# Up-products with 512-column and 256-column matmuls in turns, in a twelve-part transformer kernel

## The reference

```python
# mlp, 4 times; w1 is 1024x4096, w2 is 4096x1024
x = x + rms_norm(sq_relu_mlp(rms_norm(x, g2), w1, w2), g3)   # jnp.square(jax.nn.relu(h @ w1)) @ w2
# ffn1 and ffn2, twice each; gate and up are 1024x2816, down is 2816x1024
x = x + 0.5 * swiglu(rms_norm_2(x, norm), w_gate, w_up, w_down)  # (silu(h @ w_gate) * (h @ w_up)) @ w_down
```

## Time and profile before

| | |
|---|---|
| median of 3 runs | 2692.18 us (2687.8 to 2705.8) |
| span of the profiled execution | 2705.3 us (0.5 under the highest run; the page gives no time outside the span) |
| PE busy | 2625.5 us (97%), 21582 matmuls |
| PEld busy | 2553.7 us (94%) |
| DVE busy | 1660.7 us (61%) |
| ACT busy | 1351.4 us (50%) |
| granted TensorE clock, mean | 0.993 |
| DMA | 451.96 MB, 167 GB/s |

### The profile page before, as it was taken

The page is one execution under the profiler, slowest core; times in us unless marked ns, Lnnn a source line. Parts: engine busy times, 40 slices in busy tenths (PEclk is TensorE's granted clock), DMA queues, the critical chain, the costliest instruction groups (busy, mean ns, idle before and its releaser), DMA issues.

```text
span 2705.3 us, 48788 instructions
## 1 busy us (share of the span) xinstructions
PE 2625.5 (97%) x21582; PEld 2553.7 (94%) x21582; DVE 1660.7 (61%) x1970; ACT 1351.4 (50%) x1663; POOL 152.2 (6%) x224
## 2 busy tenths in 40 slices
PE   8989999999998999989999999999999999999998
PEld 8979999899997999988999999989999999999998
DVE  5657655475575754676755665766665657764664
ACT  5645545454436544663544444554545446544543
POOL 4400000000000000330000000000000000000000
PEclk9999999999999999999999999999999999999999
DMA  7514564456643565442565756434766655334663
GB/s 214 162 33 141 187 234 133 152 176 211 211 144 121 179 219 186 144 147 94 171 216 178 191 187 211 152 125 141 196 194 187 189 199 159 126 130 142 188 188 125
DMA packets 429970, 451.96 MB, mean 167 GB/s; under 512 B 13346, under 2 KB 395024, under 8 KB 427584
## 3 DMA queue, kind: packets, MB, share of 16 engines
q1 hardware_dynamic: 417952, 416.12, 49.2%
q0 software_dynamic: 7312, 32.35, 3.5%
q10 hardware_dynamic: 4496, 0.39, 0.1%
HBM read 441.21 MB, written 7.60 MB: 166 GB/s over the span
## 4 chain that ended last, share of the span: by engine, by line
PE 85%; DVE 6%; ACT 4%; POOL 2%; DMA 1%; issue 1%; ACTq 0%; SPq 0%; DVEq 0%
PE ps L593 85%; ACT wH L1440 2%; DVE wL L2064 2%; POOL arena L497 1%; ACT hidden_parts L1500 1%; PE ps L1037 0%; POOL arena L499 0%; DMA ring<-in_gdn_w_in 0%; DVE arena L2484 0%; DMA arena<-tiles_out 0%; DVE arena L2592 0%; DMA arena<-leaf_out 0%; DMA leaf_out<-arena 0%; POOL arena L507 0%; DVE arena L2335 0%
## 5 line engine op out<-in xcount | busy, mean ns | idle before, releaser
L2064 DVE TENSOR_TENSOR wL<-ring,wH 128x2048 fp32r<-128x2048 f32 x392 | 898.4, 2292 | 781.2 <-ACT wH L1440 780.8
L1440 ACT ACTIVATE wH<-ring 128x2048 fp32r<-128x2048 f32 x392 | 752.4, 1919 | 1050.6 <-PE ps L593 1048.6
L593 PE MATMUL ps<-hidden_parts,wH 128*128 128x256 f32 x6656 | 1005.0, 279 | 4.1 <-ACT hidden_parts L1500 2.7
L593 PEld LDWEIGHTS ps<-hidden_parts,wH 128*128 128x128 f32 x6656 | 910.8, 188 | 6.1 <-issue 3.6
L593 PE MATMUL ps<-hidden_parts,wL 128*128 128x256 f32 x3328 | 700.4, 279 | 1.0 <-DVE wL L2064 1.0
L593 PEld LDWEIGHTS ps<-hidden_parts,wL 128*128 128x128 f32 x3328 | 525.4, 188 | 1.4 <-DVE wL L2064 1.4
L593 PE MATMUL ps<-hH,wH 128*128 128x256 f32 x2624 | 369.5, 282 | 7.1 <-DVE hH L2081 5.0
L593 PE MATMUL ps<-hH,wL 128*128 128x256 f32 x2624 | 361.6, 279 | 2.2 <-DVE wL L2064 2.2
L593 PEld LDWEIGHTS ps<-hH,wH 128*128 128x128 f32 x2624 | 331.4, 189 | 16.6 <-issue 15.9
L593 PE MATMUL ps<-hL,wH 128*128 128x256 f32 x2624 | 347.0, 278 | 0.0
L593 PEld LDWEIGHTS ps<-hH,wL 128*128 128x128 f32 x2624 | 329.2, 189 | 2.9 <-DVE wL L2064 2.8
(11 more groups left out here) (301 smaller groups left out, 1965.2 us busy)
## 6 DMA issues: line engine op xcount, KB each, us to landing
ring<-in_mlp_w SPq DMA_DIRECT2D x128, 1024.0 KB, 5.4
ring<-in_ffn_w_gate SPq DMA_DIRECT2D x88, 512.0 KB, 3.9
ring<-in_ffn_w_up SPq DMA_DIRECT2D x88, 512.0 KB, 5.2
ring<-in_ffn_w_down SPq DMA_DIRECT2D x44, 1024.0 KB, 5.0
ring<-in_gdn_w_in SPq DMA_DIRECT2D x32, 1024.0 KB, 5.9
ring<-in_w_in SPq DMA_DIRECT2D x28, 1024.0 KB, 5.4
hidden_parts<-mem_parts POOLq DMA_DIRECT2D x14, 1024.0 KB, 7.5
ring<-in_mlstm_w_in SPq DMA_DIRECT2D x12, 1024.0 KB, 5.2
```

Source lines behind the costliest of these rows:

```text
L593: return pe.matmul(o, l, r, start=start, stop=stop, **k)
L1440: f(wH[:, n % PARTS, :], ring[:, n % RING, :], ACT.Copy).then_inc(sem("high_split"), 1)
L2064: tt(wL[:, n % PARTS, :], ring[:, n % RING, :], wH[:, n % PARTS, :].bitcast(F32), ALU.subtract)\
```

## The change

Units 2 and up of the up-products go through one new function, `wide_product`. For each output m and each k it issues one matmul of wH's slice with 512 moving columns (xH and xL of chunk k side by side, a view of two pieces), into a whole PSUM bank, and then one of wL's slice with xH (256 columns) into the first half of that bank. So a unit has 16 matmuls of 512 columns and 16 of 256, and 32 weight loads in place of 48. A unit takes two banks, (0,1), (6,7) or (4,5) in turn. The two halves of a bank must still be added: ScalarE copies the xL halves of both banks into SBUF, and VectorE adds the xH halves to it. The wait for `low_split` moves to the head of the unit. In mlp the square of the Relu becomes a separate VectorE instruction on SBUF data. In ffn the scaling reads SBUF data. The wait for the filler's bank (6) moves from unit 2 to unit 3, and down-products wait until the unit before the last has been read. `hH` and `hL` become one tensor `normed`. At the start, the constants' first DMA and x share a semaphore, and the step semaphores are made when first used; the order of the work is not changed by that.

```diff
-        hH = sb("hH", [P, DC, T], F32R)
-        hL = sb("hL", [P, DC, T], F32R)
+        normed = sb("normed", [P, 2, DC, T], F32R)
+        hH, hL = normed[:, 0, :, :], normed[:, 1, :, :]
...
+        def wide_banks(j):
+            return (0, 6, 4)[(j - 2) % 3]
+
+        def both_sums(j):
+            v = ps[:, wide_banks(j):wide_banks(j) + 2, :]
+            return v[:, :, 0:T], v[:, :, T:2 * T]
...
+            def wide_product(u, j, high_of, low_of, x):
+
+                for m in range(2):
+                    bank = wide_banks(j) + m
+                    halves = two(ps[:, bank, :])
+                    if m == 0:
+                        pe.wait_ge(sem("low_split"), u + 1)
+                    for k in range(DC):
+                        mm(halves, high_of(k, m), x[:, :, k, :], k == 0, False, skip_group_check=True)
+                        last = mm(ps[:, bank, 0:T], low_of(k, m), x[:, 0, k, :], False, k == DC - 1,
+                                  skip_group_check=True)
+                last.then_inc(sem("products_done"), 1)
...
                 for j in range(2, 16):
-                    if j == 2:
+                    if j == 3:
                         filler_out(filled_before[("mlp", i)])
-                    to_channels("mlp_w1", i, j, bank_of(j), free="bank_read")
+                    if j == 4:
+                        pe.wait_ge(sem("hidden_squared"), W.next("hidden_squared", 2))
+                    if j >= 5:
+                        pe.wait_ge(sem("bank_read"), W.next("bank_read"))
+                    u = slab_no[("mlp_w1", i, j)]
+                    wh, wl = high(u, DC), low(u, DC)
+                    wide_product(u, j, lambda k, m: columns(wh, k, m), lambda k, m: columns(wl, k, m), normed)
                     if i == 0 and j == 3:
                         summed_norm(3, "xsq_summed")
+                W.next("hidden_squared", 14)
+                pe.wait_ge(sem("bank_read"), W.next("bank_read", 2))
...
+                    if n == 3:
+                        filler_out(filled_before[(kind, l)])
+                    if n == 4:
+                        pe.wait_ge(sem("units_scaled"), W.next("units_scaled", 2))
+                    if n >= 5:
+                        pe.wait_ge(sem("bank_read"), W.next("bank_read"))
                     u = slab_no[(kind, l, n)]
                     wh, wl = high(u, 2 * DC), low(u, 2 * DC)
-                    if n == 2:
-                        filler_out(filled_before[(kind, l)])
-                    if n >= 4:
-                        pe.wait_ge(sem("bank_read"), W.next("bank_read"))
-                    for half in range(2):
-                        last = three(ps[:, 4 + n % 4, half * T:(half + 1) * T],
-                                     [lambda k: wh[:, half * DC + k, :], lambda k: wl[:, half * DC + k, :]],
-                                     [lambda k: ffn_x[0][:, k, :], lambda k: ffn_x[1][:, k, :]], DC,
-                                     low_weights(u, (1, 0)) if half == 0 else None)
-                    last.then_inc(sem("products_done"), 1)
+                    wide_product(u, n, lambda k, m: wh[:, m * DC + k, :], lambda k, m: wl[:, m * DC + k, :], ffn_both)
+                W.next("units_scaled", 20)
+                pe.wait_ge(sem("bank_read"), W.next("bank_read", 2))
                 down_product(f"{kind}_w_down_2", l, 22, range(22))
...
-                    f(act_s[:, g % 2, :], ps[:, 4 + g % 4, :], ACT.Relu).then_inc(sem("act_ready"), 1)
+                    src = two(ps[:, 4 + g, :]) if g < 2 else both_sums(g)[1]
+                    f(two(act_s[:, g % 2, :]), src, ACT.Copy).then_inc(sem("act_ready"), 1)
...
+                    if n >= 2:
+                        f(two(sum_s[:, n % 2, :]), both_sums(n)[1], ACT.Copy).then_inc(sem("act_ready"), 1)
...
-                    tt(prod_s[:, g % 2, :], act_s[:, g % 2, :], ps[:, 4 + g % 4, :], ALU.mult)\
-                        .then_inc(sem("bank_read"), 1)
+                    src = act_s[:, g % 2, :]
+                    if g >= 2:
+                        tt(two(src), both_sums(g)[0], two(src), ALU.add).then_inc(sem("bank_read"), 1)
                     if g >= 1:
                         hidden_low(g - 1)
+                    if g >= 2:
+                        dve.wait_ge(sem("bank_read"), W.next("bank_read"))
+                    stt(prod_s[:, g % 2, :], src, 0.0, src, ALU.max, ALU.mult).then_inc(sem("hidden_squared"), 1)
...
-                    tt(two(act_s[:, n % 2, :]), two(ps[:, 4 + n % 4, :]), rs_twice(), ALU.mult)\
-                        .then_inc(sem("bank_read"), 1)
-                    dve.wait_ge(sem("bank_read"), W.next("bank_read"))
+                    src = ps[:, 4 + n, :] if n < 2 else sum_s[:, n % 2, :]
+                    if n >= 2:
+                        dve.wait_ge(sem("act_ready"), W.next("act_ready"))
+                        tt(two(src), both_sums(n)[0], two(src), ALU.add).then_inc(sem("bank_read"), 1)
+                        dve.wait_ge(sem("bank_read"), W.next("bank_read"))
+                    tt(two(act_s[:, n % 2, :]), two(src), rs_twice(), ALU.mult).then_inc(sem("units_scaled"), 1)
+                    dve.wait_ge(sem("units_scaled"), W.next("units_scaled"))
```

More of the change, by code:

```diff
@@ L206, in __init__ @@
             def __init__(self, eng, step):
-                self.eng, self.seen, self.step, self.steps = eng, {}, sem(step), 0
+                self.eng, self.seen, self.step, self.steps = eng, {}, step, 0
             def next(self, name, n=1):
@@ L216, in mark @@
                 self.steps += 1
-                ins.then_inc(self.step, 1)
+                ins.then_inc(sem(self.step), 1)
                 return self.steps
             def chain(self, ins):
-                self.eng.wait_ge(self.step, self.mark(ins))
+                self.eng.wait_ge(sem(self.step), self.mark(ins))
         def group(name, layer, j, g=0):
@@ L288, in program @@
         gate_s = A.take(2 * T, "p (b n) -> p b n", b=2)
+        sum_s = A.take(2 * 512, "p (b n) -> p b n", b=2)
         A = Arena()
@@ L330, in program @@
         memH, memL = hidden_parts[:, 0, 24:32, :], hidden_parts[:, 1, 0:8, :]
-        ffn_x = (hidH[:, 24:32, :], hidL[:, 24:32, :])
+        ffn_both = hidden_parts[:, :, 24:32, :]
+        ffn_x = (ffn_both[:, 0, :, :], ffn_both[:, 1, :, :])
         cross_x = [flat_parts[:, at:at + DC * T].rearrange("p (c t) -> p c t", c=DC)
@@ L391, in _ @@
         def _(sp):
-            sp.dma_start(ident, io["shape_constants"][:, 0:P]).then_inc(sem("ident_in"), 16)
+            sp.dma_start(ident, io["shape_constants"][:, 0:P]).then_inc(sem("x_in"), 16)
             sp.dma_start(x_rows, io["x"][0].rearrange("(i p) n -> p i n", p=P)).then_inc(sem("x_in"), 16)
@@ L869, in ffn @@
                 for n in range(2, 22):
+                    if n == 3:
[3 more added lines that the diff above has]
+                    if n >= 5:
+                        pe.wait_ge(sem("bank_read"), W.next("bank_read"))
                     u = slab_no[(kind, l, n)]
                     wh, wl = high(u, 2 * DC), low(u, 2 * DC)
-                    if n == 2:
-                        filler_out(filled_before[(kind, l)])
-                    if n >= 4:
-                        pe.wait_ge(sem("bank_read"), W.next("bank_read"))
-                    for half in range(2):
-                        last = three(ps[:, 4 + n % 4, half * T:(half + 1) * T],
-                                     [lambda k: wh[:, half * DC + k, :], lambda k: wl[:, half * DC + k, :]],
-                                     [lambda k: ffn_x[0][:, k, :], lambda k: ffn_x[1][:, k, :]], DC,
-                                     low_weights(u, (1, 0)) if half == 0 else None)
-                    last.then_inc(sem("products_done"), 1)
+                    wide_product(u, n, lambda k, m: wh[:, m * DC + k, :], lambda k, m: wl[:, m * DC + k, :], ffn_both)
+                W.next("units_scaled", 20)
+                pe.wait_ge(sem("bank_read"), W.next("bank_read", 2))
                 down_product(f"{kind}_w_down_2", l, 22, range(22))
-                pe.wait_ge(sem("bank_read"), W.next("bank_read", 4))
+                pe.wait_ge(sem("bank_read"), W.next("bank_read"))
             def outputs(heads, values):
@@ L1403, in turn_in @@
                     last.then_inc(sem(name), 1)
-            pe.wait_ge(sem("ident_in"), W.next("ident_in", 16))
             pe.wait_ge(sem("ones_set"), W.next("ones_set"))
-            pe.wait_ge(sem("x_in"), W.next("x_in", 16))
+            pe.wait_ge(sem("x_in"), W.next("x_in", 32))
             turn_in(x_rows, "x_turned")
@@ L1593, in hidden_high @@
             def hidden_high(g):
-                act.wait_ge(sem("bank_read"), W.next("bank_read"))
+                act.wait_ge(sem("hidden_squared"), W.next("hidden_squared"))
                 f(hidH[:, 2 * g:2 * g + 2, :], two(prod_s[:, g % 2, :]), ACT.Copy).then_inc(sem("hiddenH_ready"), 1)
@@ L1598, in gate_unit @@
                 def gate_unit(n):
```

(2 more changed lines are left out.)

3 lines of the change are left out of this document (1 added, 2 removed).

## The result

The changed kernel took 2737.55 us (median of 4 runs, 2733.62 to 2742.2) against 2695.67 for the kernel before (4 runs, 2687.8 to 2705.8): a ratio of 1.0154, 95% interval 1.0125 to 1.0183. It is slower by some 42 us, where 17 less were forecast. The forecast has the wrong sign, and the result lies outside its range.

The account below looks back on a forecast made before the run. PE was taken as the bound, busy 97% of the span. Terms of -35, +11.6 and +3.6 gave -20 us on the profiled 2705.3 (2685), or -17 from the median 2692.2: 2675 us, range 2650 to 2710.

Parts of the forecast that it names:

- PE, steady: Up-products: three matmuls (one k, one m) become two, 0.328 us in fast phases, 0.333 in slow; gain 35 us.
- (a): Rival, up-products: 512 columns cost two spacings, so the gain is 0 and 2707 us results; chance 0.17.
- (b): Rival, ffn: VectorE becomes the bound, only mlp's 14 us are gained, about 2693 us; chance 0.06.
- (c): Rival, up-products: slow spacing vanishes and the narrow step is load-bound, giving 2665 us; chance 0.18.
- (d): Rival: loads run beside nothing, so 2176 loads worth 243 us go, giving 2449 us; chance 0.01.
- The heads: Head of each up-product phase: PE waits for wL ahead of unit 2, costing 11.6 us, bounds 8 and 16.
- The ends: Ends of the up-product phases: added work delays wL of the third down slab; cost 3.6 us, between 1 and 7.
- The other engines: ScalarE and VectorE in the units: VectorE 93 us more, ScalarE 47 more, free while their turns fit a unit.
- From the profile to the median: Whole kernel: profiled execution lies 13 us above the median, 3 us less to gain; 2685 on the span becomes 2675.
- The luck in the untouched phases: Untouched phases, such as mlp's down-products: spacing may fall differently, some 8 us of either sign.
- The two spacings: PE's matmuls, 0.1133 or 0.1177 us apart: two ways load and matmul fall in step, which a short wait can switch.

Follow-up runs that it names:

- stream_alone: Small separate kernel, only matmul streams on PE with the other engines idle, computes none of the reference: 0.1200 us for 256 fp32r columns, 0.2267 for 512.
- the wait alone: Kernel before, with only the wait for wL moved to the head of each unit: 2713.43 us against 2701.22, ratio 1.0037.
- grouped: Changed kernel with eight wide matmuls of wH, then eight narrow ones of wL, the wL wait only ahead of these: 2705.78 us, ratio 0.9998 to before.
- turns_shift_76: Changed kernel with wH and wL moved by 12 bytes, 76 from the activations: 2724.77 us, ratio 1.0075 to the kernel before.

## Why the prediction was wrong

**The step that failed** is "PE, steady", in its new price of a triple: "0.215 for the wide one ... then one ordinary spacing", 0.328. Measured is 0.3533, 0.025 more. By the single starts in the changed kernel the wide one has 0.235, 0.020 over its term, and the narrow one 0.1183, 0.005 over the fast spacing. The wide term was half of the earlier trace rows's 0.430, which is the columns and next to nothing else (512 at 26.7 ns per 64 are 0.2133), because fp32's rows have a fixed part of only 2.4 ns. fp32r has 13.3 ns a matmul in `stream_alone`, which a wide one pays like a narrow one: alone it takes 0.2267, 0.0117 over the term. At the 64 bytes between activations and weights that this kernel has, it takes 0.2333 among its like, 0.018 over the term. That is most of the 0.025, and the rest comes with the turns. What makes the fixed part, and why it depends on the address, stays open. With 0.3533 the slow phases gain nothing (0.353 before) and the fast ones lose 1088 x 0.0133 = 14.5 us, where 35 were to be won. That step is off by 35 + 14.5 = 49.5 us; the whole sum on the profile is off by 47 (26.6 more measured, 20 less forecast), as the other terms nearly cancel.

**The rival that came nearest** was (a), "wide costs only twice narrow": two fast spacings are 0.2267, and the wide one alone is just that. Its bound, "-5 in the fast ... phases if the narrow step is always slow", was too narrow, since the wide one in turns also stood at 0.235. Its time of 2707 and the range's end of 2710 left that out. The rivals (b), (c) and (d) are out: VectorE keeps 1.24 us idle, the slow spacing did not vanish but spread, and taking 2176 loads away saved nothing.

**The heads:** 11.6 us forecast, 10.0 measured, 9.6 with the wait alone. mlp 1 waits 1.72 where 1.75 was read from the earlier trace rows (they give 1.74). Right, except for mlp 0: the 1 us added for slab 4's split did not come as a wait, while the half clock behind its head wait, some 1.5 us, was not foreseen.

**The ends:** 3.6 forecast, 3.9 measured with the spacing held, 0.7 in each ffn (0.75 forecast for a fast one). Right.

**The other engines:** VectorE +89 us (93 forecast), its turn 4.41 (4.45); ScalarE +38 (47). Free, as said.

**From the profile to the median.** Forecast were 10 us less for the median than for the sum made on the span; measured, the median of the changed kernel stands 5.7 above its profiled span (a run is 1.7 us longer than its span). With the 47 this makes the 62 us between 2675 and 2737.55. The 10 were a draw, not a property of the kernel: how far the profiled execution of before lay over its median. The luck in the untouched phases was put at 8 us; the table shows it at 4 either way (down +4.4, rest -4.5, the transfer in it).

**The two spacings** were taken as two ways to fall in step that a short wait can switch. The waits are not what decides them: with the addresses at 76 bytes every phase was fast, with the same kind of waits. At 64 bytes both occur, in the streams too, and what chooses there is open.

## What to carry to other kernels

Measure the shape that the change brings, alone, before pricing it: here the price taken from fp32 rows missed a fixed 13.3 ns for each matmul, and the 2176 loads taken away from under a busy PE bought nothing. Where matmuls follow each other without a gap and PE bounds, the distance of weights and activations in SBUF is a setting to scan: 12 bytes of shift were worth 1% (0.9904, 2673.38 us, the fastest kernel of this study, 64 us under the changed one), and 64 bytes of shift cost 2%. Scan it in the whole kernel, as one distance serves all its products at once, and as 88 bytes were fast in the streams and not in every phase of the kernel. And look at what a new wait does to the clock behind it, as well as at its length.

## What the runs showed of the hardware that was not expected

- An fp32r matmul of n columns on 128 rows stood at n/2.4 ns + 13.3 ns (256 to 512 columns, 448 a little off) at a granted clock of 1.00, with weights and activations 0 bytes apart (modulo 256), and as low as 6.7 ns over its columns (0.1133 for 256) at some other distances.
- The same stream ran at 0.1133 to 0.122 us a matmul by the distance of its two operands, 4 bytes deciding: 72 bytes 0.118, 76 bytes 0.1133, 80 bytes 0.119. What does this no run shows.
- A wide and a narrow one in turns cost 0.3533 in the changed kernel, grouped 0.3467 at the same addresses; by distance the turns went from 0.3464 to 0.3655. The traffic of the other engines made no stream slower.
- A pause of PE of 1.79 us was followed by a granted clock of 0.50 in mlp 0 of the changed kernel, and by 1.00 in mlp 1 behind 1.72 us. In `turns_shift_76` the same pause of 1.79 us was followed by the low clock in mlp 0 and 3 and not in mlp 1 and 2.
- The kernel before spread over 2688 to 2720 us in all its runs; shifted by 12 bytes, with every phase fast, it kept to 2673.1 to 2678.4 in five. That its spread is the draw between the two spacings is likely, and not shown run by run, as only one run of each has a profile.
